# Two-block sequence model: where one weight slab is split, who scales the first head's keys, and the order of the first states

## What is computed

```python
def _gla_chunked(q, k, v, log_a):
    # one direction of GLA: S_t = diag(a_t) S_{t-1} + k_t v_t^T, o_t = S_t^T q_t
    def step(state, inp):
        q_c, k_c, v_c, b_c = inp
        ...
        o = einsum('bhid,bhde->bhie', q_c * exp(b_c), state) + einsum('bhij,bhje->bhie', scores, v_c)
        state = exp(b_last[:, :, 0, :])[..., None] * state + einsum(
            'bhjd,bhje->bhde', k_c * exp(b_last - b_c), v_c)
        return state, o

def _mixer_gla(h, w_in, gate_w2, gate_b, norm_g, w_out):
    ...
    o_f = _gla_chunked(q, k, v, log_a[0])
    o_b = _flip(_gla_chunked(_flip(q), _flip(k), _flip(v), _flip(log_a[1])))
    o = _rmsnorm(o_f + o_b, norm_g) * silu(r)
    return matmul(o, w_out)
```

## Time and profile before

| | |
|---|---|
| median of 3 runs | 1809.57 us (1807.15 to 1812.96) |
| the profiled execution, its own time | 1809.57 us |
| its span, first to last instruction | 1807.8 us |
| TensorE busy | 1772.7 us (98%) |
| VectorE busy | 1114.5 us (62%) |
| ScalarE busy | 824.5 us (46%) |
| GpSimd busy | 239.3 us (13%) |
| granted TensorE clock, mean | 0.998 |

### The profile page before, as it was taken

One profiled execution on the slowest core, in us unless ns is written; L12 is line 12 of the kernel. 1 busy time (PEld: TensorE's weight loads), 2 busy tenths in 40 slices (PEclk: granted clock), 3 DMA queues, 4 the chain that ended last, 5 costly groups with the idle time before them and its releaser, 6 DMA issues. The chain is left out here.

```text
span 1807.8 us, 25253 instructions
## 1 busy us (share of the span) xinstructions
PE 1772.7 (98%) x9832; PEld 1478.7 (82%) x9832; DVE 1114.5 (62%) x1573; ACT 824.5 (46%) x1381; POOL 239.3 (13%) x234
## 2 busy tenths in 40 slices
PE   8999999999999999999999999999999999999999
PEld 6887789888889998877887778789988877876677
DVE  4775366666588756666522468688846676533763
ACT  4433455555335654334452454236753354544540
POOL 2001133433000000010000244000010000101600
PEclk9999999999999999999999999999999999999999
DMA  5333100000132344333132200232354343330001
GB/s 162 93 93 93 47 13 13 1 1 1 61 95 96 99 133 156 120 122 106 58 93 93 70 1 1 94 94 94 117 179 136 105 140 111 128 117 24 24 1 70
DMA packets 102553, 147.17 MB, mean 81 GB/s; under 512 B 5073, under 2 KB 70817, under 8 KB 102192
## 3 DMA queue, kind: packets, MB, share of 16 engines
q1 hardware_dynamic: 95472, 121.45, 21.1%
q0 software_dynamic: 6976, 24.27, 4.1%
HBM read 143.61 MB, written 2.10 MB: 81 GB/s over the span
## 5 line engine op out<-in xcount | busy, mean ns | idle before, releaser
L279 DVE TENSOR_TENSOR wlo<-raw,whi 128x1024 fp32r<-128x1024 f32 x166 | 199.1, 1236 | 279.1 <-ACT whi L273 278.7
L300 PE MATMUL bk<-act_hi,whi 128*128 128x512 f32 (+1 forms) x880 | 324.0, 368 | 0.3 <-DVE wlo L762 0.3
L302 PE MATMUL bk<-act_hi,wlo 128*128 128x512 f32 (+1 forms) x880 | 321.1, 365 | 0.0
L301 PE MATMUL bk<-act_lo,whi 128*128 128x512 f32 (+1 forms) x880 | 321.0, 365 | 0.0
L300 PE MATMUL bk<-whi,act_hi 128*128 128x512 f32 x768 | 305.2, 397 | 6.2 <-DVE act_lo L505 5.0
L302 PE MATMUL bk<-whi,act_lo 128*128 128x512 f32 x768 | 304.8, 397 | 0.0
L301 PE MATMUL bk<-wlo,act_hi 128*128 128x512 f32 x768 | 302.8, 394 | 0.0
L273 ACT ACTIVATE whi<-raw 128x1024 fp32r<-128x1024 f32 x166 | 168.7, 1055 | 254.2 <-PE bk L302 212.7
L300 PEld LDWEIGHTS bk<-act_hi,whi 128*128 128x128 f32 x880 | 165.8, 188 | 31.2 <-issue 1.1
L301 PEld LDWEIGHTS bk<-act_lo,whi 128*128 128x128 f32 x880 | 165.9, 188 | 29.6 <-issue 1.0
L302 PEld LDWEIGHTS bk<-act_hi,wlo 128*128 128x128 f32 x880 | 165.8, 188 | 29.4
(11 more groups left out here) (442 smaller groups left out, 3124.5 us busy)
## 6 DMA issues: line engine op xcount, KB each, us to landing
raw<-in_mlp_w SPq DMA_DIRECT2D x100, 512.0 KB, 4.2
raw<-in_a_w_in SPq DMA_DIRECT2D x32, 512.0 KB, 4.1
work<-in_mlp_w SPq DMA_DIRECT2D x28, 512.0 KB, 4.4
work<-in_w_mod POOLq DMA_DIRECT2D x24, 512.0 KB, 3.9
raw<-in_b_w_in SPq DMA_DIRECT2D x24, 512.0 KB, 3.9
raw<-in_w_in SPq DMA_DIRECT2D x14, 512.0 KB, 4.1
raw<-in_a_w_out SPq DMA_DIRECT2D x8, 512.0 KB, 3.7
raw<-in_b_w_out SPq DMA_DIRECT2D x8, 512.0 KB, 4.1
```

Source lines behind the costliest of these rows:

```text
L279: nc.vector.tensor_tensor(wlo[b][:, hs], src[hf][:, :], whi[b][:, hs], ALU.subtract).then_inc(w_ready, 1)
L300: nc.tensor.matmul(acc, lhs_hi, rhs_hi, start=first, stop=False, skip_group_check=True)
L301: nc.tensor.matmul(acc, lhs_hi, rhs_lo, start=False, stop=False, skip_group_check=True)
L302: return nc.tensor.matmul(acc, lhs_lo, rhs_hi, start=False, stop=last, skip_group_check=True)
```

## The change

It has three parts. The work on every element stays the same.

1. The split of pair 32, b = 1 leaves the place before head 0. On ScalarE its two halves stand behind the last operation of head 1 and of head 2 (`act_b_head`), on VectorE behind the query of level 4 of head 2 and of head 3 (`dve_b_head`). With this, in head 0 the exponentials of units 10 and 11 stand ahead of the copy to `ktok` on ScalarE.
2. In head 0 alone, the two products `b_e(d, 7) * ktok` are made by VectorE (`dve_b_state_key`), behind the query of level 0 and ahead of merge 3, and no longer by GpSimd.
3. In all heads VectorE does decayed query 0, state 0, decayed query 1, state 1; before it did decayed query 0, both states, decayed query 1.

```diff
--- before.py
+++ after.py
@@ -2217,8 +2217,6 @@
                     wait_sum(act, "b_v", half, st)
                     nc.scalar.activation(b_v[:, st, half * 512:half * 512 + 512], bk[4 * half + st][:, :], ACT.Copy
                                          ).then_inc(sum_added, 1)
-            split_hi(act, next_pair("b_v", 1), 1)
-            act_b_token_key(act, 0)
 
         def act_b_gate_weights(act):
             act.wait_ge(B["w_loaded"], 16)
@@ -2357,8 +2355,9 @@
             if h == 0:
                 for l in (1, 2, 3, 4):
                     pool_b_key(pool, h, l)
-            for d in range(2):
-                pool_b_state_key(pool, h, d)
+            if h > 0:
+                for d in range(2):
+                    pool_b_state_key(pool, h, d)
             for l in range(5 if h == 0 else 3, LEVELS):
                 pool_b_key(pool, h, l)
             if h + 1 < BH:
@@ -2511,6 +2510,8 @@
         def act_b_head(act, h):
             for r in range(12 if h > 0 else 10, UNITS):
                 act_b_unit(act, UNITS * h + r)
+                if h == 0 and r == 11:
+                    act_b_token_key(act, h)
                 if r in (15, 19):
                     act_b_last_decay(act, h, (r - 15) // 4)
             if h + 1 < BH:
@@ -2534,6 +2535,8 @@
             nc.scalar.activation(BB["rs"], bk[7][:, :], ACT.Ln, bias=RMS_EPS, scale=1.0 / BDV).then_inc(B["o_ln"], 1)
             act.wait_ge(B["o_ln"], h + 1)
             nc.scalar.activation(BB["rs"], BB["rs"], ACT.Exp, scale=-0.5).then_inc(B["o_rs"], 1)
+            if h in (1, 2):
+                split_hi(act, next_pair("b_v", 1), 1, (h - 1,))
 
         def dve_b_norm(dve, h):
             dve.wait_ge(B["o_rs"], h + 1)
@@ -2564,8 +2567,13 @@
                 dve.wait_ge(B["st"], n)
                 nc.vector.copy_predicated(BB["ST"], bc_mat(b_masks[:, SCORES[j], :]), src).then_inc(B["st"], 1)
 
-        def dve_b_state(dve, h, cc):
-            for d in range(2):
+        def dve_b_state_key(dve, h, d):
+            dve.wait_ge(B["k_tok"], h + 1)
+            dve.wait_ge(B["exp"], UNITS * h + 11 + d)
+            nc.vector.tensor_tensor(b_e(d, 7), b_e(d, 7), BB["ktok"].rearrange("p c s -> p (c s)"), ALU.mult).then_inc(B["kd"], 1)
+
+        def dve_b_state(dve, h, cc, directions=(0, 1)):
+            for d in directions:
                 dve.wait_ge(B["u"], 6 * h + 2 * cc + d + 1)
                 s_, u = BB[f"S{d}"], bk[7 - d][:, 0:BDV]
                 if cc == 0:
@@ -2581,16 +2589,19 @@
             dve_b_query(dve, h, 3)
             dve_b_merge(dve, h, 1)
             dve_b_query(dve, h, 4)
-            if h == 0:
-                split_lo(dve, next_pair("b_qk", 5), 1)
+            if h > 1:
+                split_lo(dve, next_pair("b_qk", 5), 1, (h - 2,))
             dve_b_merge(dve, h, 2)
             dve_b_query(dve, h, 0)
+            if h == 0:
+                for d in range(2):
+                    dve_b_state_key(dve, h, d)
             if h > 0:
                 dve_b_norm(dve, h - 1)
             dve_b_merge(dve, h, 3)
-            dve_b_query_decay(dve, h, 0)
-            dve_b_state(dve, h, 0)
-            dve_b_query_decay(dve, h, 1)
+            for d in range(2):
+                dve_b_query_decay(dve, h, d)
+                dve_b_state(dve, h, 0, (d,))
             dve_b_merge(dve, h, 4)
             dve_b_query(dve, h, 5)
             if h + 1 < BH:
```

## The result

The change makes the kernel slower: 1812.04 us in the median against 1808.82 for the kernel before, both of 22 runs. The ratio is 1.0018, with a 95% interval of 1.0011 to 1.0025, so 2.0 to 4.5 us are lost. The forecast was 1809.3 us with no measurable change.

The account below looks back on a forecast made before the run. TensorE, busy 98% of the span, was taken as the bound, so only its waits count. From 1809.57 us, 2.7 gained in head 0 and 2.5 lost in heads 2 and 3 gave 1809.4, stated as 1809.3; range 1806.5 to 1812.8.

Parts of the forecast that it names:

- What bounds the kernel: TensorE is busy 98% of the span; only its waits count, two in head 0 of together 2.5 us, 0.14%.
- Head 0: Waits ahead of unit 12 and `update(0)` go: 1.3, 1.29 and some 0.1 us, 2.7 gained; bounds 1.2 to 3.2.
- The order of states: Heads 1 to 3: same four operations in the same stretch, `state_out(1)` needs the last either way; nothing taken.
- Heads 2 and 3, the split on VectorE: No slack ahead of merge 3, so the split delays TensorE: 1.25 us lost per head, 2.5 in both.
- The working guess: Heads 2 and 3, VectorE: split ends at 1088.75, merge 2 at 1089.4, query 0 at 1090.0 against 1088.9 before.
- The third rival: Full blocking: VectorE's split waits out key 4, then takes 1.22 us; 0.4 more per head, 1810.1 us; chance 0.10.
- What query 0 gives back: Heads 2 and 3: query 0, 1.58 us before, then lies behind GpSimd's work and takes nearer 0.67; 0.9 is contention.
- its bound: Heads 2 and 3: split at 1.76 us on VectorE in series with ScalarE's delay, a ceiling of 2.3 us lost per head.
- The split on ScalarE: Heads 2 and 3: unit 14 waits 0.55 us anew, hidden while VectorE's delay is longer; otherwise the floor per head.
- The transfers: Next weight halves load into `raw` later, but 22 us of cover remain before ScalarE reads the slab; nothing taken.
- the second one: Heads 2 and 3: VectorE's split at 1.76 us, ScalarE's 0.55 in series; 1811.5 us, decides from 1.35 per head; chance 0.17.

Follow-up runs that it names:

- e1: Kernel before with part 1 alone (splits moved to heads 2 and 3; GpSimd's decayed keys and old state order kept): ratio 1.0024, +4.3 us.
- e2: Kernel before with parts 2 and 3 alone, the split left whole before and in head 0: ratio 0.9996, -0.7 us against the kernel before.
- e5b: Changed kernel with splits moved to idle places in heads 0 and 1, and part 3 undone (old state order): ratio 0.9986 to the kernel before.
- e6b: Changed kernel with VectorE's split halves in heads 2 and 3 behind query 0 instead of query 4: ratio 1.0003 to the kernel before, +0.5 us.
- e7b: Changed kernel with GpSimd's key 5 of each head held until decayed query 0 is done: ratio 1.0008 to the kernel before, +1.4 us.
- e4: Changed kernel with ScalarE's split halves moved behind the next head's log decays in heads 1 and 2, VectorE's kept: ratio 1.0022 to the kernel before.
- e9: Changed kernel, splits in idle places of heads 0 and 1, key 5 held for both decayed queries, key 6 for the low part: 1804.92 against 1809.86 us.

## Why the prediction was wrong

**What bounds the kernel**, and the scale: right. The gains and losses in the heads show as waits of TensorE, and no kernel here lies over 4.5 us from the one before.

**Head 0**: right. 2.7 us were forecast, 2.63 measured. The two parts came out at 1.43 for the 1.3 forecast (e1) and at 1.23 for 1.29 (e2), so part of the agreement is luck. The 0.1 us put down to the order of the states is not there (e5b). The decayed keys took 1.26 us for two, as assumed.

**The order of states**: taken at nothing. That holds where VectorE keeps up (e5b). In heads 2 and 3 it cost 0.3 us each (e1 against the change).

**Heads 2 and 3, the split on VectorE**: here the prediction failed. That there is no slack ahead of merge 3 was right. But the term of 1.25 us per head, 2.5 in all, measured 2.28 and 2.26 with the split alone (e1) and 2.59 with the order of the states on top. Three errors lie in it:
- *The split's own time beside GpSimd.* The working guess shared the time between the engines and took it at 2.0 us (1086.75 to 1088.75); it was 2.30, as if it had waited out key 4. The third rival had this at 0.10. Moved to where GpSimd is idle it took 1.20 (e6b), and the head lost 1.32. No run held key 4 with the split left in its place, so for the split the cause rests on the moved place.
- *What query 0 gives back.* I took it at 0.67 us alone, from the fastest of all queries. It takes 1.09 beside nothing, so only 0.5 of its 1.58 could come back, not 0.9. The minimum of a line that holds the queries of seven levels is not the price of each.
- *What the delay meets next.* This was not in the sum at all. VectorE arrives at decayed query 0 with key 5 just ahead of it: 1.72 us and not 0.66. With key 5 held (e7b) this is 0.67 again, and the head 0.6 us shorter. The shares of the three don't add up, as each edit that takes one meeting away brings about another.

At merge 3 the head is 1.69 us late (8.42 us behind score 1, against 6.73 from the earlier trace rows with score 1 of before at 1083.26). Decayed query 0 adds 1.06, and some of it comes back by the first decay unit of the next head: 2.59.

The rows held a sign that full waiting was the rule, and the prediction misread it. It took key 3 in head 2 to end at 1086.48, half of the 2.98 of two keys, and found query 4 too short for a full wait. But key 3 alone is not half of the two. A view of 1085 to 1086 us of the kernel before shows it by itself:

```profile
1084.99 1.29 POOL L2349 TENSOR_TENSOR work<-work,arena 128x512 f32<-128x512 f32 x1
```

It ends at 1086.28, and query 4 ends 0.55 us behind it, at 1086.83: nearly a whole wait and then nearly the 0.67 us of an undisturbed query. The longest split of the kernel before, the 1.76 us from which the prediction took its bound, shows the same:

```profile
1683.94 1.27 POOL L3195 TENSOR_TENSOR arena<-arena 128x512 f32<-128x512 f32 x1
1684.53 1.76 DVE L279 TENSOR_TENSOR wlo<-raw,whi 128x1024 fp32r<-128x1024 f32 x1
```

GpSimd had 0.68 us left when that split was issued, and the split ended 1.08 us behind it. In the change 1.22 us of key 4 were left, and the split again ended 1.08 behind. So the 1.76 was no bound: it had met a shorter rest.

**The split on ScalarE**: right in kind. Unit 14 came 0.35 us later behind score 2, for the 0.55 forecast, and that was hidden (e4).

**The transfers**: right. The next split on ScalarE still waits for TensorE and not for the load, 4.03 us as in the earlier trace rows:

```profile
1146.71 2.01 ACT L273 ACTIVATE whi<-raw 128x1024 fp32r<-128x1024 f32 x2 [4.03 <-PE bk L302]
```

**The rivals**: the second one, slower because the split costs more per head than head 0 gives, is what happened, from its point of 1.35 us on. Its mechanism was half right: the split was slow beside GpSimd, slower than the 1.76 given as its most; ScalarE's part in series, its other half, was refuted by e4. The third rival had the right rule, but its price of 1810.1 stopped at merge 3, too: neither query 0's 1.09 nor decayed query 0's 1.72 was in it.

On that point the Trainium skill (SBUF — State Buffer, Who interferes with whom) has the rule that decides this case: "Issue order, not op shape, decides who blocks." The trace agrees for the split (2.30 us, ended 1.1 behind key 4), for decayed query 0 (1.72 behind key 5) and for the low part (2.28 behind key 6), each back at its own time when GpSimd held still. One meeting, told in the last section, went the other way although GpSimd's row began first. The prediction weighed the rule at one place only and did not carry it on to the next meeting of the two engines.

## What to carry to other kernels

Ahead of moving work to an engine, look for its idle time in the timeline and not for its share of busy time: VectorE had 2.3 us behind merge 7 with GpSimd silent, ScalarE 5.8 behind its log decays (head 0 of the kernel before), and there the same split cost nothing. Where two engines disturb each other, price a moved instruction by who is running when it arrives, and then follow the delay to the next place where they meet. Holding back the engine that is not urgent can be worth more than the move itself, but the whole run of meetings has to be arranged: one held key moved the collision to a worse place, and two left it only at query 5, which takes 1.10 us and makes score 6 come 0.28 us later (1.15 us behind the start of `update(1)` in head 1 of e9, against 0.87 in head 1 of the change).

## What was not expected of the hardware

- A difference in arrival of under 0.1 us decides over 1 us. Decayed query 0 took 0.66 us where GpSimd's row began 0.03 us ahead of it (head 1 of the changed kernel: 1060.36 and 1060.39) and GpSimd's two keys took 3.51; it took 1.72 where GpSimd began 0.11 us ahead (1090.28 and 1090.39), and the two keys took 2.95. Query 4 took its 1.77 us with key 3 only 0.07 us ahead.
- VectorE's instructions that read a bank kept their time beside GpSimd: merge 2 of head 2 took 0.73 us beside key 4, and the copy of a state 0.41 beside key 6 (1092.03 in the change).
- The query of level 0, which takes its elements singly in turn from two places, takes 1.09 us for 512 columns with GpSimd idle. The query of level 5 takes 0.67. That the pattern is the reason was not tried.
